# Mixer of a two-block network on one core: two z gate units laid between the levels, their gate function in the inverse

## The chip, the core and the metric

One NeuronCore of one Trainium2 chip. The metric is the device time of one launch in microseconds. Everything runs in one program on five engines: TensorE (PE), VectorE (DVE), ScalarE (ACT), GpSimd (POOL) and SyncE (SP), which issues the weight transfers.

## The reference

A first block of two layers (swiglu, attention of several kinds, memory attention, swiglu), which the change leaves alone, and a second block of two layers, each a mixer and a convolved gated feed-forward, on 256 tokens of width 1024, all in float32. The mixer, cut to what matters here:

```
p = h @ w_in                                   # qkv, z, beta, a, hq, hf, hi, hgate, gate_dn, gate_hg
o_dn = delta_rule(q, k, v, beta, g) forward + backward      # chunked; the triangular inverse t_inv of (a + eye)
o_dn = rmsnorm(o_dn) * dn_norm * silu(z)
o_hg = hgrn2(silu(hq), kk, hi, logf) forward + backward     # decays over all pairs of tokens
o_hg = rmsnorm(o_hg) * hg_norm * silu(hgate)
merged = sigmoid(gate_dn) * (o_dn @ w_branch_dn) + sigmoid(gate_hg) * (o_hg @ w_branch_hg)
return merged @ w_out
```

## The kernel before

**Weights** come as a stream of 324 units of 1 MB (128 x 2048 floats) through a ring of three slots. Every unit is split in two halves: ScalarE rounds a half into `w_hi` (`split_half`, L1340), VectorE subtracts it from the original into `ring_lo` (L1813), and TensorE multiplies high by high, high by low and low by high: 48 matmuls of 256 columns a unit. `feed(u)` on either engine splits unit u+2. ScalarE may write half h of unit u+2 only when TensorE has consumed half h of unit u; SyncE loads unit u+3 when unit u is used up. `features` (L754) yields columns turned, half by half; `tokens` (L767), used for hi, hz and z, needs both halves.

**Banks.** Results land in four PSUM banks taken in turn. A tile is opened only when the tile four before it has been read (`take` on ScalarE, L1305; `gather`, `conv_qkv` and others on VectorE). The order of tiles is written by `Plan.stages` and must be the order in which TensorE makes them.

**The mixer** (`mixer2`, once in each engine's program, l = 0 and 1). Each engine runs its list in the order of the text; semaphores join them. TensorE's order:

- projections: qkv and hf in turn, hq, hi, hz (hgate); then the square sums of q and k (L1125) and the sums of the decays (L1133); then the two z units. ScalarE takes z through silu (`silu_tokens`, L1624).
- the levels k = 0 to 8 (`LEVELS` is 7): for each k, VectorE builds two exponent arguments (`args(l, k)`, L2301 and L2303) over 1024 columns each, ScalarE exponentiates (L1634), GpSimd multiplies with the queries (`qmul`, L2692), TensorE multiplies per head (L1078), VectorE puts the result where a mask says (`gather`, L2332). Beside each level runs a part of the delta rule's preparation (`prepare(k)`): decay rows at 0 and 1, the Gram matrix at 2 (L2419), k and v turned at 3 (`kv_T`, L1088), query-key products at 4 (L2428). GpSimd masks matrices in `decays_of` (L2697, L2698) and `masked` (L2704), and multiplies hz and z by their norm gains (`row_gains`, L2682). Between levels one gate unit is laid (`GATE_AT`), eight in all, split in halves.
- the substitution: the inverse of the 16 x 16 diagonal blocks, in 14 rows one after the other. `near_start` on VectorE sums strided columns (L2435, four instructions) and starts it; `near_row(c)` on TensorE (L1159) and `near_step(c)` on VectorE (L2447, L2448) alternate, each waiting for the other. Rows lie after halves of gate units from (3, 0) on and after levels 4 to 8. `level_masks(NEAR)` on GpSimd waits for `near_start`.
- the inverse by levels 4 to 6: W0, Y and Z (L1078, L2490). At the last one ScalarE applies the sigmoid to the gates (L1761, 4096 columns). Then the state chain, `branch_hg` (L1269), `branch_dn`, `out_proj`.

`near_start` stands at `half == 1 and k == 2`: after `gather(2)`, the Gram products, `args(l, 4)` and one split, ahead of `gather(3)`. `args(l, 1)` stands after the split for hz1.

## Time and profile before

| | us |
|---|---|
| median of 3 runs | 2311.51 |
| lowest, highest | 2311.47, 2316.66 |
| the profiled execution | 2303.78 |
| its span | 2301.6 |
| TensorE busy | 2184.7 |
| VectorE busy | 1566.2 |
| ScalarE busy | 1064.4 |
| GpSimd busy | 191.6 |

Busy times are of the whole span, most of which the change does not touch. The two mixers' level loops lie at 1380 to 1473 us and 1898 to 1991 us. An engine's idle time in a row is followed by the instruction that ended it.

### The profile page before, as it was taken

To read this page: it belongs to the slowest core of one execution; us is meant where nothing else is said; L and a number is where in the kernel's file an instruction comes from. 1 tells how busy PE (TensorE), PEld (TensorE's weight loads), DVE (VectorE), ACT (ScalarE), POOL (GpSimd) and SP (SyncE) were. 2 spreads that over 40 slices of the span, in tenths; PEclk is the share of its full clock that TensorE was granted. 3 is DMA by queue.
4 is the path that set the end of the run, shared out by engine and by line. 5 is a ranking of instruction groups with operands and counts; after the bars stand their busy time and mean duration, and the time that the engine had idled before them with its cause. 6 is when DMAs were issued, how large, how long until landed. Compare 5 with 4: busy or idle time off the path is not lost.

```text
span 2301.6 us, 39173 instructions
## 1 busy us (share of the span) xinstructions
PE 2184.7 (95%) x15722; PEld 2038.9 (89%) x15722; DVE 1566.2 (68%) x2330; ACT 1064.4 (46%) x1504; POOL 191.6 (8%) x157
## 2 busy tenths in 40 slices
PE   7999989999999999999998998999999998999997
PEld 7998859989999998798997988898998988898996
DVE  4557657656575575667556689867767689867676
ACT  4335465533353345554333475434434475434442
POOL 0000000131000000000001007300000007300000
PEclk9999999999999999999999999999999999999999
DMA  6554424475555554344553442214554442214553
GB/s 251 188 182 165 165 74 165 153 214 184 208 194 187 188 191 146 128 147 166 185 191 139 165 147 92 74 56 149 190 189 167 165 147 92 74 62 168 183 183 126
DMA packets 52665, 359.10 MB, mean 156 GB/s; under 512 B 6400, under 2 KB 6784, under 8 KB 11072
## 3 DMA queue, kind: packets, MB, share of 16 engines
q1 hardware_dynamic: 46928, 340.81, 41.3%
q0 software_dynamic: 4336, 13.37, 2.1%
q10 hardware_dynamic: 1280, 3.19, 0.4%
q8 instruction: 91, 1.49, 0.3%
q14 instruction: 30, 0.25, 0.0%
HBM read 356.29 MB, written 1.05 MB: 155 GB/s over the span
## 4 chain that ended last, share of the span: by engine, by line
PE 79%; DVE 11%; ACT 4%; DMA 4%; issue 2%; SPq 0%; DVEq 0%; POOLq 0%; ACTq 0%
PE tile L754 43%; PE acc L787 18%; PE tile L767 7%; PE tile L1078 3%; DMA ring<-weights 3%; DVE ring_lo L1813 2%; PE tile L1269 2%; ACT w_hi L1340 2%; PE tile L923 1%; PE tile L897 1%; PE tile L802 1%; DVE work L2332 1%; DVE work L2303 1%; DVE bn L2198 0%; DVE work L2301 0%
## 5 line engine op out<-in xcount | busy, mean ns | idle before, releaser
L1813 DVE TENSOR_TENSOR ring_lo<-ring,w_hi 128x1024 fp32r<-128x1024 f32 x648 | 788.6, 1247 | 594.1 <-ACT w_hi L1340 591.9
L1340 ACT ACTIVATE w_hi<-ring 128x1024 fp32r<-128x1024 f32 x648 | 657.7, 1053 | 913.8 <-DMA ring<-weights 706.2
L754 PE MATMUL tile<-xT_hi,w_hi 128*128 128x256 f32 x3008 | 859.3, 286 | 25.7 <-DVE xT_lo L1804 13.9
L754 PE MATMUL tile<-xT_lo,w_hi 128*128 128x256 f32 x3008 | 854.2, 284 | 0.0
L754 PE MATMUL tile<-xT_hi,ring_lo 128*128 128x256 f32 x3008 | 854.0, 284 | 0.0
L754 PEld LDWEIGHTS tile<-xT_hi,w_hi 128*128 128x128 f32 x3008 | 580.3, 193 | 33.7 <-DVE ring_lo L1813 17.0
L754 PEld LDWEIGHTS tile<-xT_lo,w_hi 128*128 128x128 f32 x3008 | 580.5, 193 | 2.1
L754 PEld LDWEIGHTS tile<-xT_hi,ring_lo 128*128 128x128 f32 x3008 | 580.2, 193 | 0.0
L787 PE MATMUL acc<-w_hi,hidden_hi 128*128 128x512 f32 x528 | 206.6, 391 | 2.0 <-DVE ring_lo L1813 2.0
L787 PE MATMUL acc<-w_hi,hidden_lo 128*128 128x512 f32 x528 | 206.1, 390 | 0.0
L787 PE MATMUL acc<-ring_lo,hidden_hi 128*128 128x512 f32 x528 | 205.5, 389 | 0.0
L1305 ACT ACTIVATE work<-tile 128x512 f32<-128x512 f32 (+2 forms) x186 | 101.0, 566 | 64.2 <-PE tile L1078 28.6
L1078 PE MATMUL tile<-work 128*128 128x128 f32 (+1 forms) x976 | 117.2, 280 | 3.8 <-issue 1.6
L1078 PEld LDWEIGHTS tile<-work 128*128 128x128 f32 x976 | 114.3, 195 | 5.0 <-issue 3.7
L787 PEld LDWEIGHTS acc<-w_hi,hidden_hi 128*128 128x128 f32 x528 | 99.4, 188 | 21.5 <-issue 2.2
L787 PEld LDWEIGHTS acc<-ring_lo,hidden_hi 128*128 128x128 f32 x528 | 99.2, 188 | 21.1
L787 PEld LDWEIGHTS acc<-w_hi,hidden_lo 128*128 128x128 f32 x528 | 99.4, 188 | 18.3
L767 PE MATMUL tile<-w_hi,xT_hi 128*128 128x256 f32 x352 | 100.2, 285 | 7.1 <-ACT work L1611 3.2
L767 PE MATMUL tile<-w_hi,xT_lo 128*128 128x256 f32 x352 | 99.6, 283 | 0.0
L767 PE MATMUL tile<-ring_lo,xT_hi 128*128 128x256 f32 x352 | 99.6, 283 | 0.0
L787 PE MATMUL acc<-w_hi,xT_hi 128*128 128x512 f32 x192 | 77.4, 403 | 2.8 <-DVE xT_lo L1804 2.8
L767 PEld LDWEIGHTS tile<-w_hi,xT_hi 128*128 128x128 f32 x352 | 67.5, 192 | 8.3 <-issue 5.0
(273 smaller groups left out, 2718.1 us busy)
## 6 DMA issues: line engine op xcount, KB each, us to landing
ring<-weights SPq DMA_DIRECT2D x324, 1024.0 KB, 4.8
work<-ln_g_rows POOLq DMA_DIRECT2D x8, 512.0 KB, 6.0
work<-ln_b_rows POOLq DMA_DIRECT2D x8, 512.0 KB, 7.2
work<-rpb POOLq DMA_DIRECT2D x32, 96.0 KB, 13.7
x<-x_in SPq DMA_DIRECT2D x1, 1024.0 KB, 8.0
work<-mem_in ACTq DMA_DIRECT2D x1, 1024.0 KB, 6.6
out<-x POOLq DMA_DIRECT2D x1, 1024.0 KB, 4.4
work<-hmask_in ACTq DMA_DIRECT2D x1, 840.0 KB, 8.3
```

Of the source, the lines that this page charges most:

```text
L754: j = mm(ps[:, f * S:(f + 1) * S], w[a][:, k, :], x2[b][:, k, :], start=(k == 0 and i == 0), stop=(k == KT - 1 and i == 2))
L767: j = mm(ps[:, tt * 256:(tt + 1) * 256], x2[b][:, k, tt * P:(tt + 1) * P], w[k // 4][a][:, k % 4, :], start=(k == 0 and i == 0), stop=(k = ...
L787: j = mm(acc[b][:, :], src[d][:, at + k, (b // 2) * P:(b // 2 + 1) * P], w[k][c][:, 0, (b % 2) * 512:(b % 2 + 1) * 512], start=(first and ...
L802: i = nc.tensor.transpose(ps[:, k * S + tt * P:k * S + (tt + 1) * P], src[:, tt, c:c + P], ident)
L897: i = mm(ps[:, tt * S:(tt + 1) * S], qs[m][:, tt * P:(tt + 1) * P], ks[m], start=(m == 0), stop=(m == len(qs) - 1))
L923: i = mm(dst, value_rows(a, e, j)[:, st, :], probT[:, e % 4, st, :], start=(st == 0), stop=(st == TT - 1))
L1078: i = mm(part(ps[:, h * P:(h + 1) * P]), lhsT(h), rhs(h), start=True, stop=True)
L1269: i = mm(ps[:, f * S:(f + 1) * S], w[c][:, k, f * P:(f + 1) * P], x2[d][:, 2 * q0 + k, :], start=(k + p == 0), stop=(k == 3 and p == 2))
L1305: A(dst, ps[:, :] if src is None else src(ps), ACT.Copy, scale=scale).then_inc(tile_taken[t % NB], 1)
L1340: A(high_of(u, h), half_of(ring, u, h), ACT.Copy).then_inc(sems["w_hi"], 1)
L1813: V.tensor_tensor(half_of(ring_lo, u, h), half_of(ring, u, h), high_of(u, h).bitcast(F32), ALU.subtract).then_inc(sems["w_lo"], 1)
L2303: V.tensor_tensor(half(Q), pairs_of(hX, 0, m, n + m), pairs_of(hX, m, m, n - 1, 0), ALU.subtract).then_inc(sems["hg_arg"], 1)
```

## The change

- The z units leave the place ahead of level 0. z0 is laid behind gate unit 2, z1 behind gate unit 5 (`Z_AT`), in the weight stream, the plan of tiles and on all engines.
- ScalarE only copies z (`take`); silu is applied to both at once, 1024 columns, in the last level of the inverse, ahead of the sigmoid. GpSimd's gains of z wait for it and come last.
- The square sums and decay sums come after hi, ahead of hz; ScalarE squares before it takes hi0. VectorE reads the decay sums before the split for hz0, scales q and k before that for hz1, and does `args(l, 1)` after it.
- `near_start` comes at `half == 0 and k == 3`, behind `gather(3)` and `args(l, 5)`. Row 1 comes after (3, 1) in place of (3, 0); the row so lost comes after z1 (`NEAR_AFTER_Z`).

```diff
-             ("hi", 0), ("hi", 1), ("hz", 0), ("hz", 1), ("z", 0), ("z", 1))
+             ("hi", 0), ("hi", 1), ("hz", 0), ("hz", 1))
-NEAR_AFTER_HALF = ((3, 0), (3, 1), (4, 0), (4, 1), (5, 0), (5, 1), (6, 0), (6, 1), (7, 0))
+Z_AT = {2: 0, 5: 1}
+NEAR_AFTER_Z = (5,)
+NEAR_AFTER_HALF = ((3, 1), (4, 0), (4, 1), (5, 0), (5, 1), (6, 0), (6, 1), (7, 0))
...
@@ TensorE
-                for name in ("hi", "hz"):
-                    for j in range(2):
-                        project(name, j)
+                for j in range(2):
+                    project("hi", j)
                 square_sums()
                 decay_sums()
                 for j in range(2):
-                    project("z", j)
+                    project("hz", j)
...
+                    if k in Z_AT:
+                        project("z", Z_AT[k])
+                    if k in NEAR_AFTER_Z:
+                        near_row(next(rows))
...
@@ ScalarE
-                for j in range(2):
-                    feed_one("hi", j)
-                    if j == 0:
-                        silu_qkv(5)
-                    take(T[("hi", l, j)], tok2(hi, j))
+                feed_one("hi", 0)
+                silu_qkv(5)
                 act.wait_ge(sems["qkv_silu"], 6 * l + 4)
                 for j in range(4):
                     A(pair(l2s, j), pair(qkvT, j), ACT.Square).then_inc(sems["l2_sq"], 1)
-                for j in range(2):
-                    feed_one("hz", j)
-                    silu_tokens(T[("hz", l, j)], tok2(hz, j))
+                take(T[("hi", l, 0)], tok2(hi, 0))
+                feed_one("hi", 1)
+                take(T[("hi", l, 1)], tok2(hi, 1))
...
                 for j in range(2):
-                    feed_one("z", j)
-                    silu_tokens(T[("z", l, j)], tok2(zs, j))
+                    feed_one("hz", j)
+                    silu_tokens(T[("hz", l, j)], tok2(hz, j))
...
+                    if k in Z_AT:
+                        feed_one("z", Z_AT[k])
+                        t = T[("z", l, Z_AT[k])]
+                        take(t, tok2(zs, Z_AT[k]), lambda ps: ps.rearrange("p (t c) -> p t c", t=TT))
...
                     if v == LEVELS - 1:
+                        for j in range(2):
+                            act.wait_ge(*taken(T[("z", l, j)]))
+                        A(zs, zs, ACT.Silu).then_inc(sems["z_silu"], 1)
                         for i in range(8):
                             act.wait_ge(*taken(T[("gate", l, i)]))
                         A(gates[:, :, :], gates[:, :, :], ACT.Sigmoid).then_inc(sems["gates_ready"], 1)
...
@@ VectorE
                 feed_one("hi", 1)
                 next(parts)
-                feed_one("hz", 0)
-                next(parts)
-                feed_one("hz", 1)
-                args(l, 1)
...
+                next(parts)
+                feed_one("hz", 0)
                 for j in range(4):
                     dve.wait_ge(sems["l2_inv"], 4 * l + j + 1)
                     V.tensor_tensor(pair(qkvT, j), pair(qkvT, j), pair(l2s, j), ALU.mult).then_inc(sems["l2_done"], 1)
-                feed_one("z", 1)
+                feed_one("hz", 1)
+                args(l, 1)
...
-                        if half == 1 and k == 2:
+                        if half == 0 and k == 3:
                             near_start()
...
+                    if k in Z_AT:
+                        feed_one("z", Z_AT[k])
+                    if k in NEAR_AFTER_Z:
+                        near_step(next(rows))
...
@@ GpSimd
+                    if name == "z":
+                        pool.wait_ge(sems["z_silu"], l + 1)
...
                 qmul(6)
-                row_gains("z", zs, 0)
                 qmul(7)
                 qmul(8)
                 level_masks(NEAR + 1)
                 level_masks(NEAR + 2)
+                row_gains("z", zs, 0)
```

## Rows read from the trace of the kernel before

**Rows 1.** The page: the chain that ended last, by engine, shares of the span.
```profile
PE 79%; DVE 11%; ACT 4%; DMA 4%; issue 2%; SPq 0%; DVEq 0%; POOLq 0%; ACTq 0%
```

**Rows 2.** TensorE's waits in 1897:1991: total, times, longest us.
```profile
PE tile L1088 <- DVE work L2332: 6.1, 1, 6.1
PE acc L1159 <- DVE work L2448: 3.5, 3, 1.6
PE tile L754 <- DVE work L2332: 2.9, 2, 2.3
```

**Rows 3.** Busy sums, level 0 to gate unit 6, both mixers; columns as headed.
```profile
core 0: us, PE busy (x) PEld busy (x) DVE busy (x) ACT busy (x) POOL busy (x), PEclk, DMA share, GB/s
1380.10:1454.40 74.30, 63.61 (x516) 62.65 (x515) 68.65 (x69) 40.37 (x55) 50.03 (x25) 0.95 0.28 98
1897.90:1972.40 74.50, 62.75 (x515) 61.79 (x515) 68.15 (x69) 40.40 (x55) 49.99 (x25) 0.95 0.28 98
```

**Rows 4.** The same columns for three stretches at a low clock.
```profile
1408.30:1411.70 3.40, 3.40 (x18) 3.40 (x17) 2.98 (x5) 0.00 (x0) 3.40 (x4) 0.50 0.00 0
1500.40:1507.30 6.90, 6.90 (x35) 6.90 (x35) 2.72 (x11) 2.68 (x5) 0.00 (x0) 0.51 0.01 2
1937.30:1944.20 6.90, 4.27 (x20) 4.28 (x21) 6.87 (x7) 1.20 (x2) 6.03 (x4) 0.51 0.01 2
```

**Rows 5.** First mixer: z in the chain (start, us); ScalarE's and TensorE's timeline.
```profile
1368.64 11.62 PE tile L767 x96
...
1348.55 0.63 ACT L1629 ACTIVATE work<-work 128x512 f32<-128x512 f32 x1 [0.16 <-DVEq L2188]
1351.37 2.01 ACT L1340 ACTIVATE w_hi<-ring 128x1024 fp32r<-128x1024 f32 x2 [1.71 <-DMA ring<-weights]
1353.76 2.18 ACT L1694 ACTIVATE l2s<-work 128x512 f32<-128x512 f32 x4
1366.55 2.42 ACT L1702 ACTIVATE l2s<-tile,small 128x512 f32<-128x512 f32 x4
...
1367.38 1.03 PE L1133 MATMUL tile<-small,const 128*128 128x4 f32 x8 [0.34 <-ACT l2s L1702]
```

**Rows 6.** VectorE's timeline in the second mixer: start, us, line, operands, count.
```profile
1898.37 2.36 DVE L1813 TENSOR_TENSOR ring_lo<-ring,w_hi 128x1024 fp32r<-128x1024 f32 x2 [1.35 <-ACT w_hi L1340]
1903.37 3.75 DVE L2303 TENSOR_TENSOR work<-work 128x1024 f32<-128x1024 f32 x1
...
1957.14 1.21 DVE L2301 TENSOR_TENSOR work<-work 128x1024 f32<-128x1024 f32 x1
...
1964.96 3.42 DVE L2301 TENSOR_TENSOR work<-work 128x1024 f32<-128x1024 f32 x1
```

**Rows 7.** GpSimd's timeline there; its first 12 rows have no gap.
```profile
1903.07 2.97 POOL L2692 TENSOR_TENSOR work<-work 128x1024 f32<-128x1024 f32 x1 [38.42 <-ACT work L1634]
...
1926.61 6.50 POOL L2704 TENSOR_TENSOR work<-work,blocks 128x512 f32<-128x512 f32 x4
1938.17 7.39 POOL L2704 TENSOR_TENSOR work<-work,blocks 128x512 f32<-128x512 f32 x4 [1.18 <-DVE work L2439]
1952.35 2.39 POOL L2692 TENSOR_TENSOR work<-work 128x1024 f32<-128x1024 f32 x1 [6.79 <-ACT work L1634]
```

**Rows 8.** VectorE's strided sums and gather(3), and TensorE's transposes and gate units.
```profile
1925.19 0.36 PE L754 MATMUL tile<-xT_hi,w_hi 128*128 128x256 f32 x1 [2.26 <-DVE work L2332]
1934.10 3.77 DVE L2435 TENSOR_REDUCE work<-work 128x64 f32<-128x512 f32 x4
1939.14 1.34 DVE L2332 COPY_PREDICATED work<-hmask,tile 128x512 f32<-128x512 uint8 x2
1939.93 1.97 PE L1088 MATMUL tile<-const,work 128*128 128x128 f32 x8 [6.09 <-DVE work L2332]
1941.55 0.56 PE L754 MATMUL tile<-xT_hi,w_hi 128*128 128x256 f32 x1
1959.97 0.46 PE L1159 MATMUL acc<-work,spread_own 128*128 128x96 f32 x2 [1.10 <-DVE work L2448]
```

**Rows 9.** ScalarE and TensorE at the end of the second mixer's inverse.
```profile
2025.12 1.28 ACT L1761 ACT_TABLE_LOAD   x1
2026.42 3.62 ACT L1761 ACTIVATE work<-work 128x4096 f32<-128x4096 f32 x1
2029.94 0.58 ACT L1305 ACTIVATE work<-tile 128x512 f32<-128x512 f32 x1
...
2030.62 0.35 PE L1078 MATMUL tile<-work 128*128 128x128 f32 x1 [0.79 <-issue]
```

More of the change, by code:

```diff
@@ L261, in stages @@
                     self.from_chip(("ba_T", l), 1)
-                if (name, j) == ("hz", 1):
+                if (name, j) == ("hi", 1):
                     self.from_chip(("l2", l), 4)
@@ L270, in stages @@
                     self.from_units(("gate", l, k), 1)
+                if k in Z_AT:
+                    self.from_units(("z", l, Z_AT[k]), 1)
             self.from_chip(("hg_o", l), 2)
@@ L387, in weight_stream @@
         out += [packed[name][j:j + 1] for name, j in PROJECTED]
-        out.append(pack_features(w[:, 4624:6672]))
+        gates = pack_features(w[:, 4624:6672])
+        for k in range(8):
+            out.append(gates[k:k + 1])
+            if k in Z_AT:
+                out.append(packed["z"][Z_AT[k]:Z_AT[k] + 1])
         out.append(pack_branch(a["w_branch_hg_2"][l]))
@@ L581, in build @@
                   "a_scaled", "a_ready", "a_near", "a_level", "near_eye", "spread", "near_x", "near_row", "x_first", "vb", "kd", "nbe",
-                  "z_ready", "dn_ssq", "dn_std", "dn_out", "gates_ready", "merged_dn", "merged"]
+                  "z_ready", "z_silu", "dn_ssq", "dn_std", "dn_out", "gates_ready", "merged_dn", "merged"]
         qs_both = region(0, 2, 4 * S)
@@ L1742, in mixer2 @@
                             take(T[("gate", l, g)], pair(gates, g))
+                    if k in Z_AT:
+                        feed_one("z", Z_AT[k])
+                        t = T[("z", l, Z_AT[k])]
+                        take(t, tok2(zs, Z_AT[k]), lambda ps: ps.rearrange("p (t c) -> p t c", t=TT))
                 for g in range(4):
@@ L2398, in mixer2 @@
                 signal(sems["gc_arg"], 1)
-                feed_one("z", 0)
+                next(parts)
+                feed_one("hz", 0)
                 for j in range(4):
@@ L2471, in mixer2 @@
                                                 ALU.mult).then_inc(sems["x_first"], 1)
+                    if k in Z_AT:
+                        feed_one("z", Z_AT[k])
+                    if k in NEAR_AFTER_Z:
+                        near_step(next(rows))
                 dve.wait_ge(*ready(T[("hg_o", l)] + 1))
```

## The prediction

> **What bounds the kernel now.** I read the page first: TensorE is busy for 2184.7 of 2301.6 us, and the chain that ended last is 79% TensorE and 11% VectorE [rows 1]. Work taken from other engines is therefore worth nothing unless TensorE waits for it; the question is where TensorE stands still inside the two mixers. The matmuls of the z units are not removed, only laid elsewhere, so a gain can come only from idle time of TensorE that they fill. The list of waits over the level loop of the second mixer gives that idle time: 6.1 us in one wait before the third kv transpose, 2.9 us in two waits before gate units, 3.5 us in three waits before rows of the substitution, 12.5 us in all, every one ended by VectorE [rows 2]. The first mixer has 5.0 in place of 6.1 and else the same. Then the sums by stretch: from the first matmul of level 0 to the first of gate unit 6 takes 74.3 us and 74.5 us; VectorE is busy 68.7 and 68.2 of them, GpSimd 50.0 [rows 3]. So this stretch belongs to VectorE as much as to TensorE: what is put into it must fit VectorE too. Last the clock: after such idle time TensorE is granted 0.5, its 1.2 GHz level in place of 2.4, for 3.4 us in gate unit 2 of the first mixer, which has only a wait of 2.3 us ahead of it, and for 6.9 us around the long wait of the second [rows 4]. At 1.2 GHz gate unit 3's first half in the second mixer lost 1.2 us.
>
> All times below are in the second mixer, counted from level 0's first matmul at 1897.86; the first differs by tenths. Each term falls twice.
>
> **What moves out in front.** A z unit is 48 matmuls; two are 11.6 us (96 in 11.62) [rows 5]. They leave the place ahead of level 0 and their 11.6 us come back inside the loop, so the loop's stretch must grow by less than 11.6 us for a gain.
>
> **The square sums go earlier: +0.6.** They now stand behind hi, with hz behind them. ScalarE, from its silu at 1349.18: squares 2.18 (to 1351.4), take hi0 0.58, split for hi1 2.01, take hi1 0.58 (1354.5), table load 1.28, first logarithm 0.6 (1356.4). TensorE ends hi1 at 1351.9 and the squares 3.6 us later at 1355.5, then waits 0.9 us for that bank; today this wait is 0.34 us [rows 5]. Cost 0.6 us. The split of the next weights stays hidden: the two hz units (11.6 us) lie over it.
>
> **The level exponents' first arguments go later: +1.2 at gate unit 2.** `args(l, 1)` was done long before level 0; now it follows the split of hz1, which ends 2.9 us after that unit's last matmul (z1 today: 1897.86 to 1900.73), and gather(0) stands behind it [rows 6]. Two instructions of 1.21 us put gather(0) from 2.8 to 5.2, so gate unit 0, which needs the bank that the gather empties, starts at 5.9 in place of 5.3. The exponent follows at 5.2 and the first product on GpSimd at 7.2 in place of 5.2. GpSimd then has no gap for 30 us [rows 7], and VectorE's two-input operations come out at 2.1 to 3.8 us instead of 1.21 wherever one of GpSimd's runs [rows 6, 7]. I carry 1.2 of the 2.0 us to gate unit 2 (bounds 0 and 2.0; the gather that releases it is behind VectorE work which has slack of about 0.8): it starts at 28.6 in place of 27.3.
>
> The Trainium skill (SBUF — State Buffer, "two separate sides") says that a VectorE operation with two SBUF inputs and a GpSimd operation exclude each other for the whole instruction. The trace agrees: the 3.75 us instruction ends 1.1 us after GpSimd's 2.97 us product. By that rule alternate operations, not shares of bandwidth, set the times of the next steps; I had the same from the rows.
>
> **z0 behind gate unit 2.** Gate 2 ends at 34.4, z0 at 40.2. Its bank is free. VectorE's split ends 2.9 later (43.1), gather(3) empties its first bank at 43.8 and ends at 44.5; the third kv transpose goes at 43.9, gate unit 3 at 45.0 against 43.7 today [rows 8]. So z0 is hidden but for 1.3 us: the 6.1 us wait is filled. This is the change's gain.
>
> **The strided sums behind gather(3): +1 more.** Today the four reductions (3.77 us) and a small subtraction stand before gather(3), under that wait; row 1 never waited. Now gather(3) ends at 44.5, args(5) is blocked once by the product of level 4 (2.2) and takes 2 x 1.2: 49.1; sums and subtraction 3.96: 53.0. TensorE is through gate 3 at 50.8 and waits 2.2 us at row 1. Level 4 starts at 53.3 against 51.0. If args(5) is not blocked there is no wait here; if both halves are, it is 4.4.
>
> **VectorE from there on.** The mask products of GpSimd (7.39 us for four) wait for those sums, so they now fall on splits and steps that ran undisturbed: split 1.2, step 1.4, split 2.1, gather 0.7 give gate unit 4 at 58.4 against 54.8. Behind the masks come level 5's product and the gains of hz (2.4 us each), over args(6), which ran free (1.21 each) [rows 6, 7]: rest of gather 0.65, step 1.0, QK products 2.5, args(6) 4.6, step 0.5: 67.6. Row 4, now at the end of gate 4, waits for that, 3.2 us, against 1.1 us today; gate 5 starts at 69.7 against 64.4. The z gains no longer fall on args(7) (3.42 us today, 1.21 free), which gives back 2.2 us of VectorE time.
>
> **z1 behind gate unit 5.** VectorE is by now behind, so little is idle to fill: gate 5 with rows 6 and 7 and 1.0 us of wait ends at 76.8, z1 at 82.6, level 6 and its row at 84.6 to 85.4, where the row waits 0.9 us for the split of z1 and the added step behind it. Gate unit 6 starts at 86.4. Against 74.5 that is 11.9 more; less the 11.6 us that left: **+0.3**. Bounds by the rows: no collision at all takes off 1.2, 2.2, 2.2 and 1.4 (about -6.5), two at each place add as much as 3.
>
> **Clock: +0.8.** The long wait goes, and with it 1.2 us lost at 1.2 GHz (2.0 in the first mixer), which is counted above as gained; but waits of 3.1 (gate 2), 2.2 and 3.2 us take its place, and 2.3 us was enough once of two times [rows 2, 4]. A fall costs 1.4 us (half of 3.4 us at half speed, less a little). Bounds 0 and 3; I take 0.8.
>
> **The silu in the inverse: +2.35.** z is now only copied; a silu over 1024 columns stands before the sigmoid of the gates. Today ScalarE, after its last take of Y, loads a table (1.28), does the sigmoid (3.62) and takes the first new rows (ends at 2030.52), and TensorE's next group starts at 2030.62 after 0.79 us of idle [rows 9]. ScalarE is already last there, so all that is added is on the path. Silu: 1.06 by the rows of other 128x1024 activations. A load of its own: every change between two such functions in the trace has one of 1.28 us, so 2.34. Bounds 1.06 (both in one table) and 2.34. What follows up to the branch is one serial chain, so nothing takes it back. GpSimd's z gains (2.4 us) now run there too and hold VectorE until about the same moment; nothing more.
>
> The Trainium skill (ScalarE: Activation LUTs, "What ACT_TABLE_LOAD costs", and its rule to batch by table set) speaks against this edit: a switch is 1.28 us plus a drain of 1.38. The trace shows the 1.28 and no drain: the sigmoid starts 0.02 us after the load. By the page the term would be 3.7 and the sum 2.8 us larger for the two mixers.
>
> **Sum.** 0.6 + 0.3 + 0.8 + 2.35 = 4.05 us a mixer, 8.1 in all. The profiled execution took 2303.8 us (span 2301.6): 2311.9. The median of the runs is 7.7 us above the profiled one; on it the forecast is **2319.6 us**. A measurement tells a change from none at about 0.3%, 7 us, so this is just on the slow side; its own range is 2314 to 2326.
>
> **Rivals.**
> 1. Faster: the gaps are really filled. If args(5), args(6) and the splits miss GpSimd's operations, the loop gains 6.5 in place of losing 0.3, and the clock stays up: 0.6 - 6.5 + 2.35 = -3.6 a mixer: 2304.4. For it: 12.5 us of waits stand there, and it needs about half of them; from 3 us on it is a gain. Against: VectorE's 68 of 74 us. It decides at row 1: a wait under 0.5 us there. Chance 0.17.
> 2. No difference: the loop comes out even, the clock stays up, and silu shares the sigmoid's table: 0.6 + 0.3 + 1.06 = 2: 2315.5. Against the last: three loads for sqrt, sigmoid, sqrt. Chance 0.30.
> 3. Slower, the clock: it falls at gate 2, at row 4 and behind the lengthened wait in the inverse (0.79 + 2.35 = 3.1 us), where the first mixer already spent 6.9 us at 0.5 [rows 4]: 1.4 + 1.4 + 1.7 more: 8.1 + 9 = 17: 2328.5. Chance 0.13.
> Forecast 0.40.
>
> Range 2303 to 2330. Slower by over 0.3% (above 2318.4): 0.6 of the forecast, rival 3, a little of rival 2: 0.42. Faster (below 2304.6): most of rival 1: 0.15. Within: 0.43.
>
> **What would show it.** Right: no wait of 5 us before the kv transposes; a wait of about 2 us for VectorE at the first row and 3 us at the fourth; level 0 to gate 6 at about 86 us; in the inverse two table loads, and the idle time before the first state product at about 3.1 us. Wrong: an idle time there under 1 us (then silu is hidden), or the loop at 80 us (then z1 was hidden too).

## The result, and the profile after

The changed kernel takes 2325.45 us in the median of 10 runs (2316.64 to 2336.84), the kernel before beside it 2311.49 us (10 runs, 2304.35 to 2316.66). The ratio is 1.0063, interval 1.0048 to 1.0078: slower by 14 us, between 11 and 18. The forecast was 8.1 us slower, 2319.6 us. The direction and the serial costs were right; 6 us are missing from the sum, and by an estimate from all runs they belong to the clock of TensorE.

The profiled executions differ by more: the span went from 2301.6 to 2324.0 us. The windows of both mixers show where. The first fence is the kernel after, in three stretches of each mixer (from hi to level 0; level 0 to gate unit 6; gate unit 6 to `branch_hg`), and ahead of them the stretch up to the first mixer's hi. Columns as in [rows 3]. In the changed kernel the line numbers are others: L762 are the gate units, L1096 the transposes, L1167 the rows of the substitution, L1086 the products of levels and states; on VectorE L2344 and L2347 are the gathers, L2451 the end of `near_start`, L2460 `near_step`.

```profile
0.00:1348.80 1348.80, 1291.93 (x9031) 1194.66 (x9031) 835.30 (x1259) 624.37 (x938) 55.73 (x85) 0.98 0.50 171
1377.40:1463.10 85.70, 74.71 (x611) 73.08 (x610) 75.05 (x76) 45.22 (x61) 49.00 (x23) 0.98 0.30 106
1463.10:1541.00 77.90, 71.82 (x565) 70.55 (x564) 51.74 (x97) 29.94 (x37) 18.06 (x11) 0.91 0.09 33
1903.30:1989.20 85.90, 74.66 (x611) 73.04 (x610) 75.01 (x76) 45.25 (x61) 48.96 (x23) 0.98 0.29 107
1989.20:2064.60 75.40, 69.09 (x564) 67.83 (x564) 51.50 (x97) 29.68 (x36) 18.07 (x11) 0.95 0.09 33
```

The kernel before, in the stretches that [rows 3] do not hold:

```profile
0.00:1340.30 1340.30, 1279.39 (x9030) 1186.32 (x9030) 834.87 (x1259) 624.19 (x938) 57.39 (x85) 0.99 0.49 172
1340.30:1380.10 39.80, 39.42 (x307) 37.21 (x308) 31.61 (x50) 29.09 (x43) 0.40 (x1) 1.00 0.43 157
1454.40:1527.50 73.10, 69.18 (x565) 67.85 (x564) 50.32 (x98) 27.44 (x34) 16.03 (x10) 0.95 0.09 32
1972.40:1990.50 18.10, 17.29 (x141) 17.04 (x141) 16.37 (x26) 5.47 (x5) 8.16 (x5) 1.00 0.18 66
1990.50:2042.20 51.70, 48.57 (x426) 47.53 (x425) 33.95 (x72) 21.64 (x29) 7.85 (x6) 1.00 0.06 22
```

- Ahead of the mixer no instruction is changed, and yet 1348.8 stands against 1340.3 us, with 12.5 us more of busy TensorE for the same matmuls: in that execution 51 us ran at the 1.2 GHz level, in the one before 24. In the 13 profiled executions of this study the stretch takes 1340.3 to 1346.8 us with the old order of the weights (3 of them) and 1340.5 to 1352.2 with the new, and on the whole it is the longer the more of it runs at 1.2 GHz (24 us in the shortest, 55 in the longest). So these 8.4 us are a difference of the clock between two executions; that the change adds to it is not shown, and the runs of the table behind experiment 8 speak against it.
- hi to level 0: 28.64 us against 39.75, which is +0.5 once the 11.6 us of z are added. The second mixer has 30.11 against 39.83, +1.9; a stretch of 3.4 us at 1.2 GHz lies in it.
- Level 0 to gate unit 6: +11.4 in both mixers against [rows 3], less the 11.6 that left: -0.2.
- Gate unit 6 to `branch_hg`: 77.85 against 73.09, and 75.37 against 69.82 us: +4.8 and +5.5.

The mixers lose 5.1 and 7.3 us, 12.3 us together, and 10.3 of it in the inverse. Another 1.7 us lie between the mixers, where after has 3.4 us at 1.2 GHz.

The inverse holds falls of the clock that the change did not bring. 44 to 45 us into the stretch TensorE waits 0.78 us for VectorE in every kernel, and up to 2.6 us later the clock falls in 18 of the 26 profiled mixers, for 6.8 or 10.2 us: in before in the first mixer ([rows 4], 1500.4) and not in the second, in after in both. They are as frequent with the silu ahead of the sigmoid (7 of 10) as without (11 of 16). Without a fall the stretch takes 69.7 to 69.8 us. Each us at 1.2 GHz costs 0.42 to 0.48 us in it, so such a fall is worth 3.2 to 3.3 us or 4.9. The one of after's first mixer:

```profile
1508.90:1515.70 6.80, 6.80 (x34) 6.80 (x34) 2.83 (x11) 2.25 (x5) 0.00 (x0) 0.50 0.01 2
```

TensorE's waits in the second mixer's loop (after), beside [rows 2]: the wait of 6.1 us before the third kv transpose is down to 0.7, and the waits have moved to the rows of the substitution.

```profile
PE acc L1167 <- DVE work L2460: 5.3, 3, 3.3
PE tile L762 <- DVE work L2347: 3.3, 2, 2.5
PE acc L1167 <- DVE work L2451: 1.9, 1, 1.9
PE tile L762 <- DVE work L2344: 0.9, 1, 0.9
PE tile L1096 <- DVE work L2347: 0.7, 1, 0.7
```

The timeline of after: row 1, row 4 and the first state product; then ScalarE ahead of that product. These answer to [rows 8] and [rows 9].

```profile
1957.60 0.41 PE L1167 MATMUL acc<-work,spread_own 128*128 128x32 f32 x2 [1.86 <-DVE work L2451]
1971.34 0.45 PE L1167 MATMUL acc<-work,spread_own 128*128 128x80 f32 x2 [3.31 <-DVE work L2460]
2053.01 0.46 PE L1086 MATMUL tile<-work 128*128 128x128 f32 x2 [3.16 <-issue]
...
2045.15 1.28 ACT L1773 ACT_TABLE_LOAD   x1
2046.44 1.06 ACT L1773 ACTIVATE work<-work 128x1024 f32<-128x1024 f32 x1
2047.52 1.28 ACT L1776 ACT_TABLE_LOAD   x1
2048.81 3.62 ACT L1776 ACTIVATE work<-work 128x4096 f32<-128x4096 f32 x1
2052.33 0.58 ACT L1316 ACTIVATE work<-tile 128x512 f32<-128x512 f32 x1
```

The wait of 3.16 us is [rows 9]'s 0.79 plus 2.37, a table load and a silu.

### The profile page after: what moved, and what is told of

Its sections match the earlier page's. It is cut to its first block, busy times and chain, and to the rows that moved or that the text cites. A ratio compares the mean times of both kernels' runs of the same rounds, so it can differ in the third digit from the quotient of the medians.

```text
span 2324.0 us, 39179 instructions
## 1 busy us (share of the span) xinstructions
PE 2206.1 (95%) x15722; PEld 2054.7 (88%) x15722; DVE 1567.8 (67%) x2330; ACT 1069.2 (46%) x1508; POOL 191.9 (8%) x157
## 4 chain that ended last, share of the span: by engine, by line
PE 77%; DVE 12%; DMA 5%; ACT 5%; issue 2%; SPq 0%; POOLq 0%; DVEq 0%; ACTq 0%
PE tile L762 43%; PE acc L795 19%; PE tile L775 4%; DMA ring<-weights 4%; PE tile L1086 3%; DVE ring_lo L1828 3%; ACT w_hi L1351 2%; PE tile L1280 2%; PE tile L931 1%; PE tile L905 1%; DVE work L2316 1%; PE tile L810 1%; DVE work L2318 1%; PE tile L918 1%; DVE bn L2213 1%
## 5 line engine op out<-in xcount | busy, mean ns | idle before, releaser
L762 PE MATMUL tile<-xT_hi,w_hi 128*128 128x256 f32 x3008 | 858.8, 286 | 25.2 <-DVE xT_lo L1819 13.9
L762 PE MATMUL tile<-xT_lo,w_hi 128*128 128x256 f32 x3008 | 854.5, 284 | 0.0
L762 PE MATMUL tile<-xT_hi,ring_lo 128*128 128x256 f32 x3008 | 854.5, 284 | 0.0
L762 PEld LDWEIGHTS tile<-xT_hi,w_hi 128*128 128x128 f32 x3008 | 580.4, 193 | 32.2 <-DVE ring_lo L1828 15.7
L762 PEld LDWEIGHTS tile<-xT_lo,w_hi 128*128 128x128 f32 x3008 | 580.4, 193 | 2.2
L762 PEld LDWEIGHTS tile<-xT_hi,ring_lo 128*128 128x128 f32 x3008 | 580.3, 193 | 0.0
L1316 ACT ACTIVATE work<-tile 128x512 f32<-128x512 f32 (+1 forms) x190 | 103.9, 567 | 72.5 <-PE tile L1086 31.1
L1086 PE MATMUL tile<-work 128*128 128x128 f32 (+1 forms) x976 | 122.5, 287 | 8.3 <-issue 6.3
L1086 PEld LDWEIGHTS tile<-work 128*128 128x128 f32 x976 | 119.6, 203 | 9.5 <-issue 8.4
L795 PE MATMUL acc<-w_hi,xT_hi 128*128 128x512 f32 x192 | 77.4, 403 | 0.0
```

The costliest lines, as they stand in the source:

```text
L762: j = mm(ps[:, f * S:(f + 1) * S], w[a][:, k, :], x2[b][:, k, :], start=(k == 0 and i == 0), stop=(k == KT - 1 and i == 2))
L795: j = mm(acc[b][:, :], src[d][:, at + k, (b // 2) * P:(b // 2 + 1) * P], w[k][c][:, 0, (b % 2) * 512:(b % 2 + 1) * 512], start=(first and ...
L1086: i = mm(part(ps[:, h * P:(h + 1) * P]), lhsT(h), rhs(h), start=True, stop=True)
L1316: A(dst, ps[:, :] if src is None else src(ps), ACT.Copy, scale=scale).then_inc(tile_taken[t % NB], 1)
```

## The experiments

Each was timed in 3 to 5 rounds against the kernel before. "Ahead" is the stretch up to hi, "clean" a stretch without time at 1.2 GHz.

**1. The change once more.** No edit.

> The changed kernel once more, unedited. In its first profile 12.3 us of the 22.4 us of longer span lay inside the two mixers (5.0 and 7.3 from the first hi unit to branch_hg) and 8.4 us ahead of them, in code that the change does not touch. Theory A (the mixers' serial work costs the time): the mixers again take 5 to 7 us each more than before, and the stretch ahead of the first mixer comes out within 2 us of the kernel before. Rival B (something in the unchanged part is slower for good, as by the other order of the weights): 8 us ahead of the mixers again. Total by A +10 to +15, by B +20.

Ratio 1.0041 (1.0025 to 1.0058), 2323.5 us. Ahead 1345.9 us, where theory A wanted 1340.3 within 2 us and rival B 8 us more: it fits neither, which suits a length that the clock sets anew each time. The mixers take +2.8 and +7.5 us against before; the first lacks the fall of 6.8 us behind the long wait that after had. The waits in the loop are the same but for row 4 (2.6 us in the first mixer, and 0.6 before gate unit 4). So the loss in the mixers repeats, within some us of the clock, and the loss ahead of them does not keep its size.

**2. Silu behind the take.** The three lines move from the last level of the inverse to between the takes of `vnA` and `vnB`, when the state products already run.

```diff
                     if v == LEVELS - 1:
-                        for j in range(2):
-                            act.wait_ge(*taken(T[("z", l, j)]))
-                        A(zs, zs, ACT.Silu).then_inc(sems["z_silu"], 1)
                         for i in range(8):
...
                 take(T[("vnA", l)], vn[:, 0, :])
+                for j in range(2):
+                    act.wait_ge(*taken(T[("z", l, j)]))
+                A(zs, zs, ACT.Silu).then_inc(sems["z_silu"], 1)
                 take(T[("vnB", l)], vn[:, 2, :])
```

> The silu over z moved on ScalarE from ahead of the sigmoid to behind the take of vnA, where ScalarE was idle for 5.6 us in the kernel before. Theory A: the wait before the first state product goes back from 3.16 us to 0.79, 2.4 us a mixer, and with it the fall of the clock behind it (up to 3 us more in a mixer that had one): 5 to 9 us faster than the changed kernel. Rival C (GpSimd's z gains and the idle time elsewhere take its place): the gap falls, but branch_hg does not start earlier by more than 1 us a mixer; under 3 us in all.

2312.59 us, ratio 0.9997 (0.9983 to 1.0011): 10.9 us less than experiment 1 on the same chip, a little more than the 5 to 9 expected. ScalarE and TensorE around that point; the load and the silu are still there, and TensorE's wait is back at 0.79:

```profile
1520.77 0.58 ACT L1316 ACTIVATE work<-tile 128x512 f32<-128x512 f32 x1
1521.37 1.28 ACT L1777 ACT_TABLE_LOAD   x1
1522.66 1.06 ACT L1777 ACTIVATE work<-work 128x1024 f32<-128x1024 f32 x1
1526.93 0.60 ACT L1316 ACTIVATE work<-tile 128x512 f32<-128x512 f32 x1 [3.21 <-PE tile L1086]
...
1521.45 1.24 PE L1086 MATMUL tile<-work 128*128 128x128 f32 x9 [0.79 <-issue]
```

In the kernel before, ScalarE was idle for 5.6 us there, and with load and silu it is still idle for 3.2, so the same work costs nothing. The place of one activation was the difference between slower and equal in the medians. Of the 10.9 us the wait explains 4.7; experiment 4 takes up the rest.

**3. The strided sums ahead of gather(3) again.** Beside it everything of the change.

```diff
-                        if half == 0 and k == 3:
+                        if half == 1 and k == 2:
                             near_start()
```

> The strided sums back at level 2, ahead of gather(3), everything else as changed. Theory A: the wait of 1.86 us at row 1 goes, GpSimd's mask products start 10 us earlier and no longer run beside the splits and args(6), so the 3.31 us wait at row 4 shrinks below 1.5; gather(3) comes at most 1.5 us later. Level 0 to gate unit 6 from 85.7 to about 82 us, 3 to 4 us a mixer, 6 to 8 us in all. Rival D (the sums had to go behind the gather because z0's place leaves no room ahead): the kv transposes wait about 4 us in place of 0.7 and the stretch stays at 85 us or grows.

2316.8 us, ratio 1.0023 (1.0007 to 1.0038), 6.7 us less than experiment 1. The loop is 81.7 and 82.6 us in place of 85.7 and 86.0. The waits of the first mixer's loop:

```profile
PE tile L762 <- DVE work L2347: 3.3, 2, 2.5
PE acc L1167 <- DVE work L2460: 2.1, 2, 1.1
PE tile L1096 <- DVE work L2347: 1.2, 1, 1.2
PE tile L762 <- DVE work L2344: 0.9, 1, 0.9
```

Row 1's wait (1.86) is gone and row 4's is 1.1 in place of 3.3; the kv transposes wait 1.15 in place of 0.70. The sums could have stayed: z0's matmuls over them left room for 3.8 us. Moving them behind the gather bought 0.4 us and cost 3.4 to 4. VectorE's busy time in the loop fell from 75.05 to 73.47 us in the first mixer and from 75.01 to 74.19 in the second, so 0.8 to 1.6 us are operations that run shorter; the rest is order.

**4. Silu alone, in the kernel before.** z is copied, its silu stands ahead of the sigmoid, GpSimd's gains come last; the z units stay ahead of level 0. A second kernel has the silu where experiment 2 puts it.

```diff
-                    silu_tokens(T[("z", l, j)], tok2(zs, j))
+                    take(T[("z", l, j)], tok2(zs, j), lambda ps: ps.rearrange("p (t c) -> p t c", t=TT))
...
                     if v == LEVELS - 1:
+                        for j in range(2):
+                            act.wait_ge(*taken(T[("z", l, j)]))
+                        A(zs, zs, ACT.Silu).then_inc(sems["z_silu"], 1)
...
-                row_gains("z", zs, 0)
                 qmul(7)
...
+                row_gains("z", zs, 0)
```

> The kernel before with one part of the change alone: z copied, the silu over both z units in the inverse ahead of the sigmoid, GpSimd's z gains last; z units stay ahead of level 0. Theory A: the wait before the first state product grows from 0.79 to 3.16 us in both mixers, 4.7 us in all, plus what a fall of the clock adds there (0 to 3 us a mixer), less about 1 us a mixer of the level loop because the z gains leave args(7) alone: +3 to +8 us against the kernel before. Rival C: within 2 us of the kernel before.

> The kernel before with z copied and its silu behind the take of vnA; z units stay ahead of level 0, sums as before. Theory A: the level loop stays at 72 us as in the run with the silu ahead of the sigmoid (2.3 us under the kernel before, because GpSimd starts earlier without the two table loads at z and the z gains leave args(7)), and the wait before the state product is back at 0.79: 2 to 2.5 us a mixer, 4 to 5 us below the kernel before. It says how much of any gain has nothing to do with the place of the z units. Rival F (those 2.3 us come from the clock): 0.

2316.45 us, ratio 1.0020 (1.0001 to 1.0039), wait 3.16 us; with the silu late 2312.87, ratio 0.9995 (0.9985 to 1.0006), wait 0.79. The first is within the expected +3 to +8; the second missed its 4 to 5 us of gain.

That expectation was read across a border. The loop, level 0 to gate unit 6, was 72 us in both, 2.4 less than before. But the kernel before waits 1.64 us for a row of the substitution just ahead of gate unit 6, and these two wait 0.91 us behind the first half of that unit instead, which is in the next stretch. Without a fall of the clock the next stretch takes 70.9 us in the kernels with that wait, and 69.8 in before. In experiment 8, second mixer:

```profile
1971.10:2042.00 70.90, 66.06 (x565) 64.58 (x564) 51.45 (x98) 30.83 (x37) 18.02 (x11) 1.00 0.11 44
```

So 1.1 of the 2.4 us only changed stretches. Of the 1.3 that remain, 0.8 are there at gate unit 2 already (26.5 us after level 0 in place of 27.3), far ahead of the gains of z: a silu at z needed a table load ahead of it and one behind it, the copy needs none, and the first exponent comes earlier. (The whole kernel has 38 loads with the silu ahead of the sigmoid, 40 before.) The second kernel's profiled execution spent 10.2 us at 1.2 GHz in each inverse besides.

Three pairs now differ in the place of the silu alone: 1.0041 to 0.9997, 1.0020 to 0.9995, and 1.0023 to 0.9976 (experiment 3 and 5). Their mean is 0.39% or 9.0 us, about 6 to 12, where the lengthened waits account for 2 x 2.37 = 4.7.

The granted clock at the end of that wait tells of the rest. Windows of this kernel (silu ahead of the sigmoid), one in each mixer; the wait ended at 1520.34 and 2042.96:

```profile
1520.50:1523.90 3.40, 3.40 (x17) 3.40 (x17) 0.69 (x1) 0.00 (x0) 0.00 (x0) 0.50 0.00 0
2042.70:2046.10 3.40, 3.14 (x15) 3.17 (x16) 0.69 (x1) 0.16 (x1) 0.00 (x0) 0.50 0.00 0
```

The kernel after, first mixer, there (the wait ended at 1526.91):

```profile
1525.90:1532.70 6.80, 5.79 (x27) 5.82 (x28) 2.15 (x5) 0.91 (x2) 0.00 (x0) 0.50 0.00 1
```

Experiment 2, both mixers, from the start of its wait of 0.79 us on, over 10.8 us:

```profile
1520.60:1531.40 10.80, 9.69 (x82) 9.32 (x82) 7.66 (x24) 4.97 (x6) 2.36 (x1) 1.00 0.01 2
2038.20:2049.00 10.80, 9.69 (x82) 9.32 (x82) 7.66 (x24) 4.98 (x6) 2.36 (x1) 1.00 0.01 2
```

Over all profiled executions: from the end of the wait of 3.16 us on (at most 1.0 us sooner) the clock stood at 1.2 GHz in 6 of 10 mixers (4 times for 3.4 us, 2 times for 6.8), behind the wait of 0.79 us in none of 16. The cost is what the stretch takes beyond a clean one (69.8 or 70.9 us), the 2.37 us and the earlier fall: 74.73 - 70.9 - 2.37 = 1.5 us in the first mixer of this kernel, 1.4 to 1.5 in the three others with 3.4 us, 2.5 in the first of after. That is 1.1 us a mixer in the mean, and the deferred silu comes to 2 x (2.37 + 1.1) = 6.9 us, which the 6 to 12 allow. The 2 us up to 9.0 are within the interval and have no cause shown.

**5. Both repairs.** Experiments 2 and 3 in one kernel.

> The changed kernel with both earlier edits at once: silu behind the take of vnA, strided sums back ahead of gather(3). Theory A (two separate serial costs): level 0 to gate 6 about 82 us as with the sums alone, gate 6 to branch_hg about 70 to 73 as with the silu alone, so each mixer 4 us shorter than with the silu alone: 184 and 183 us, against 187.2 and 184.2 of the kernel before. Total 3 to 6 us below the kernel before. Rival E (the clock takes it back): the sum of the two gains, 11 and 7 us, does not appear, since falls of the clock just move; within 2 us of the kernel before.

2307.99 us, ratio 0.9976 (0.9961 to 0.9991): with the silu late and the sums early, the kernel is 4.4 us faster than before in the medians, as theory A expected. In the profile the first mixer took 183.4 us, as forecast; the second 189.0, with 20.5 us at 1.2 GHz in it.

**6. The arguments of level 1 ahead of the split for hz1.** First in the changed kernel, then in experiment 5's.

```diff
-                feed_one("hz", 1)
                 args(l, 1)
+                feed_one("hz", 1)
```

> The changed kernel with args(l, 1) ahead of VectorE's split for hz1, nothing else. Theory A (my step of the prediction: 0.6 us at gate 0, 1.2 us by gate 2): the wait before gate 0 goes from 0.85 to 0, gate unit 2 starts 1 to 1.5 us earlier after level 0, level 0 to gate 6 from 85.8 to about 84.6; 2 to 3 us in all below the changed kernel. Rival G: under 1 us, as the waits before gates 1 and 2 grow in its place (they did, by 0.6 and less, where the sums were early too).

> As the run with both edits, and args(l, 1) ahead of VectorE's split for hz1. Theory A: gather(0) comes 2.4 us earlier, the 0.9 us wait before gate 0 goes, GpSimd starts 1.3 to 2 us earlier; 1 us a mixer, 2 us in all, below the run with both edits. Rival G (gate 2 is released by VectorE's own work): the wait before gate 0 goes and the one before gate 2 grows by as much; within 1 us.

2322.98 us (1.0037; 1.0025 to 1.0049), which is not to be told from experiment 1, as rival G had it; and 2302.52 us (0.9964; 0.9950 to 0.9978), 5.5 us less than experiment 5. What the loop shows is smaller: the wait at gate unit 0 is gone (0.85 to none), but where gate 1 still waits it is 1.4 to 1.5 in place of 0.85, and gate unit 2 starts at 28.0 in place of 28.8 in the first one's second mixer. From hi to gate unit 6 that is 109.8 us against 110.4 in the first mixers, 111.3 against 112.9 in the second. So the order is worth 0.5 to 1.6 us a mixer. Of the rest the clock has a part: the runs of this kernel spent 7 us less at 1.2 GHz than those of experiment 5 (table below), which is worth 2 us.

**7. z1 ahead of level 0.** On top of experiment 6's second kernel: z1 is projected after hz1, as before, z0 stays behind gate unit 2, and the rows have their old places. One thing more differs, which "as that run" in the expectation passes over: `args(l, 1)` stands where the kernel before has it, behind the split for hz1 and ahead of the one for z1.

```diff
-Z_AT = {2: 0, 5: 1}
-NEAR_AFTER_Z = (5,)
-NEAR_AFTER_HALF = ((3, 1), (4, 0), ...
+Z_AT = {2: 0}
+NEAR_AFTER_Z = ()
+NEAR_AFTER_HALF = ((3, 0), (3, 1), (4, 0), ...
...
@@ VectorE
-                args(l, 1)
                 feed_one("hz", 1)
+                args(l, 1)
+                feed_one("z", 1)
```

> As that run, but z1 stays ahead of level 0 and only z0 lies in the loop; the rows of the substitution lie as in the kernel before. Theory A (behind gate 5 VectorE is the bound and z1 fills nothing): 5.8 us move from the loop to the stretch ahead and the mixer keeps its length within 1 us, or gets shorter by up to 2. Rival H (z1 does fill the 1.64 us wait that stood there): 1.6 us a mixer longer.

> The kernel with z1 ahead and z0 behind gate 2 once more, for a second measurement beside the run with both in the loop: 0.995 to 0.997 of the kernel before, mixers of 182 to 184 us in the profile apart from falls of the clock.

2304.51 us, ratio 0.9957 (0.9941 to 0.9973), and once more 2302.55 us, 0.9955 (0.9939 to 0.9971). The first mixer of the first one, hi to level 0 and level 0 to gate unit 6, both clean:

```profile
1347.10:1381.50 34.40, 33.65 (x259) 31.41 (x260) 29.40 (x48) 26.36 (x40) 0.40 (x1) 1.00 0.41 151
1381.50:1454.80 73.30, 66.51 (x564) 65.55 (x563) 69.34 (x71) 41.58 (x58) 48.36 (x23) 1.00 0.30 103
```

Together 107.7 us, where z1 behind gate unit 5 made 109.8. But not these 2.1 us are z1's. The wait of 0.91 us before a row falls behind the border here, as in experiment 4, and takes 1.1 us with it into the next stretch. And gate unit 2 starts 27.3 us after level 0, as in the kernel before, in place of 28.2; the arguments stand a unit further ahead of level 0 here. From hi to `branch_hg`, with a clean inverse, it is 178.6 us here (178.9 and 179.8 in two mixers with 3.4 us at 1.2 GHz in the loop) against 179.5 there, also with 3.4 us: the mixer keeps its length within 1 us, as theory A had it, and which of the two places is better for z1 is not shown. VectorE is busy for 69.3 of the loop's 73.3 us here.

z0 is the part that pays. The second kernel of experiment 4 has both z units in front (39.92 + 71.87 = 111.8) and the same border; against it 3 to 4 us a mixer are gone (the two differ in z0's place and the orders in front).

**8. z0 behind gate unit 1, z1 behind gate unit 2.** Again on top of experiment 6's second kernel, with its order of the arguments and splits; neither z unit stands in front.

```diff
-Z_AT = {2: 0, 5: 1}
-NEAR_AFTER_Z = (5,)
-NEAR_AFTER_HALF = ((3, 1), (4, 0), ...
+Z_AT = {1: 0, 2: 1}
+NEAR_AFTER_Z = ()
+NEAR_AFTER_HALF = ((3, 0), (3, 1), (4, 0), ...
```

> With the silu late, the sums early and args(l, 1) early: z0 behind gate unit 1 and z1 behind gate unit 2, rows as in the kernel before. GpSimd, not VectorE or TensorE, paces levels 0 to 3 (no gap in its work for 30 us), so a unit there costs only VectorE's two splits. Theory A: the waits before gate 2 (2.26 us) and the kv transposes (1.3 to 2.8) are filled by z0, stretch hi to gate 6 from 107.9 us (z1 ahead) to about 105.5: 2 us a mixer, 4 in all, below the kernel with z1 ahead. Rival H: VectorE's splits of z0 meet GpSimd's operations at 2.1 us each, gather(2) and with it gate 2 come 4 us later, and nothing or less than nothing is left of it.

2304.84 us, ratio 0.9958 (0.9940 to 0.9975). The second mixer, hi to level 0 and level 0 to gate unit 6, and its waits in the loop:

```profile
1865.10:1893.70 28.60, 27.84 (x210) 25.61 (x211) 24.98 (x45) 23.96 (x37) 0.40 (x1) 1.00 0.40 142
1893.70:1971.10 77.40, 72.40 (x611) 71.43 (x611) 75.55 (x75) 44.02 (x61) 48.73 (x23) 1.00 0.33 111
```

```profile
PE tile L1096 <- DVE work L2347: 2.7, 1, 2.7
PE acc L1167 <- DVE work L2460: 1.9, 2, 1.0
PE tile L762 <- DVE work L2347: 1.3, 1, 1.3
```

106.0 us, 1.7 less than in experiment 7: the wait of 2.3 us ahead of gate unit 2 is filled, while the kv transposes still wait 2.7. VectorE is busy for 75.6 of 77.4 us, so there is little left to fill. The 4 us in all that theory A expected did not come: in the medians the two cannot be told apart.

**All runs, with their clock.** Each run's span and mean granted clock c are on record, and 2 x (1 - c) x span is its time at 1.2 GHz. In the 190 runs, a us more of that time goes with 0.31 us more of span within a kernel (a line through the runs of each, with one slope for all; 0.30 in the 77 runs of before alone). That takes a difference apart: "at equal clock" is what remains when 0.31 us for each us at 1.2 GHz is taken off; it is an estimate, good to about 1.2 us. An asterisk marks mixers in which 1.1 us lie behind the border at gate unit 6.

| kernel | ratio to before | us at 1.2 GHz, mean of the runs | us against before, at equal clock | profile: hi to gate unit 6, first and second mixer (us at 1.2 GHz) |
|---|---|---|---|---|
| before | 1 | 77 | 0 | 114.1 (6.8), 114.4 (6.8) |
| after | 1.0063 | 92 | +8.6 | 114.4 (3.4), 116.1 (6.8) |
| 1, after again | 1.0041 | 84 | +7.9 | 114.6 (3.4), 116.3 (6.8) |
| 2, silu late | 0.9997 | 67 | +2.9 | 114.8 (3.4), 117.3 (10.2) |
| 3, sums early | 1.0023 | 87 | +2.1 | 110.3 (3.4), 112.7 (6.8) |
| 4, z in front, silu ahead of the sigmoid | 1.0020 | 85 | +3.2 | 111.8 (6.8)*, 112.2 (6.8)* |
| 4, z in front, silu late | 0.9995 | 84 | -2.2 | 111.8 (6.8)*, 111.8 (6.8)* |
| 5, both | 0.9976 | 75 | -3.8 | 110.4 (3.4), 112.9 (6.8) |
| 6, after with the arguments early | 1.0037 | 87 | +6.4 | 113.4 (6.8), 118.1 (13.7) |
| 6, both and the arguments early | 0.9964 | 68 | -5.7 | 109.8 (3.4), 111.3 (6.8) |
| 7, z1 ahead | 0.9957 | 71 | -7.6 | 107.7 (0)*, 108.1 (3.4)* |
| 7, again | 0.9955 | 70 | -7.1 | 108.9 (3.4)*, 109.2 (3.4)* |
| 8, z behind 1 and 2 | 0.9958 | 78 | -8.9 | 107.6 (3.4)*, 106.0 (0)* |

The kernels of experiments 5, 6 (its second), 7 and 8 beat both kernels, by 0.2 to 0.4% on the one before. The silu's three pairs differ by 5.0, 5.4 and 5.9 us at equal clock (the waits: 4.7), and by 17, 0.5 and 12 us at 1.2 GHz.

## Why the prediction was right, and where its size was off

- **z0 hidden but for 1.3 us; the long wait filled.** Right in the mechanism: the kv transposes wait 0.7, and the value of z0 there is 3 to 4 us a mixer (experiment 7). Gate unit 3 started at 46.5 (45.0 forecast, 43.7 before); the 1.5 us are a fall of the clock in gate unit 2, 3.4 us long.
- **The square sums, +0.6.** Right: +0.5 in the clean front; their bank's wait is 0.7.
- **Gate unit 2 at 28.6.** Measured 28.8, behind a wait of 2.5 us (3.1 forecast). Gate unit 0 started at 6.4 (5.9 forecast). The arguments' own part of it was less than the 1.2 us forecast: putting them early gave back 0.6 to 0.8 at gate unit 2 (experiment 6).
- **Row 1 waits 2.2, row 4 3.2, row 9 0.9.** Measured 1.86, 3.31 and 0.97 to 1.17. Row 4 started at 68.0 (67.6 forecast), gate unit 6 at 85.7 and 86.0 (86.4). The loop's +0.3 was -0.2. (The bound of this step with no collision, "about -6.5", adds up to 0.3 - 7.0 = -6.7; nothing hangs on it.) The alternation of GpSimd's and VectorE's two-input operations, from which these followed, shows in the fence below this list: the first half of `args(5)` took 3.25 us beside a product of GpSimd, the second, of the same shape and free of it, 1.21. The Trainium skill (SBUF — State Buffer, "two separate sides") gives the exclusive lock as the reason; the trace agrees in these two numbers. How much of experiment 3's 4 us comes from such meetings is not shown apart from the 0.8 to 1.6 us by which VectorE's busy time fell.
- **The silu, +2.35.** The wait grew by 2.37, and all of it was on the path. The Trainium skill (ScalarE: Activation LUTs, "What ACT_TABLE_LOAD costs") would have added a drain of 1.38 us; here each function started 0.01 to 0.02 us after its load of 1.28, and the wait has no room for a drain. The prediction also had the rule of the Trainium skill to batch by table set (ScalarE: Activation LUTs, "Table sets: the hidden batching unit") speak against this edit. The count of loads says otherwise: with the silu deferred and nothing else changed there are 38, against 40 before, one less in each mixer. What cost was the place of the load and the silu, ahead of a product that waits for ScalarE; experiment 2 has both and no such wait.
- **The step that failed: the size of "Clock: +0.8".** The prediction counted 1.2 us (2.0 in the first mixer) of the long wait's fall as gained in the loop and put 0.8 us for new falls beside it, all in the loop; for the inverse it said that nothing more comes. In the loop that was not too little: there was one stretch of 3.4 us a mixer, less than before's 6.8. What the runs showed in its place are falls elsewhere. In the inverse the wait of 3.16 us is followed by 1.2 GHz in 6 of 10 mixers, worth 1.1 us a mixer. The forecast had this only in its third rival, at 1.7 us, with a chance of 0.13; for this place it was the likelier case. And in the front of the second mixer the clock fell for 3.4 us in 6 of the 8 kernels with both z units out of it, +1.5 us, not foreseen. The price of a fall was right: 1.4 us for 3.4 us forecast, 1.4 to 1.5 measured.
- **The sum with these sizes:** 8.1 - 1.6 (the clock of the loop) - 1.0 (the loop, twice 0.5) + 2.2 (the inverse) + 1.5 (the front) = 9.2 us. Experiment 1, the second measurement of the same kernel, gave 9.5 us (6 to 13); the first gave 11 to 18.
- **Where the rest of the 14 us lies.** In the clock, by the estimate in the table above. At equal clock the change costs 8.6 and 7.9 us in its two measurements, which is what its serial costs add up to: front 0.5, loop -0.2 and about 1.4 more for its 3.4 us less at 1.2 GHz, silu 2.37, twice: 8.1. The forecast without its clock had nearly the same, 2 x (0.6 + 0.3 + 1.2 + 2.35) = 8.9, with the 1.2 us counted as gained put back, so it took the clock to give back 0.8 us in all. Instead the runs of after spent 15 us more at 1.2 GHz than those of before, worth 4.7 us, and those of experiment 1 spent 7 us more, worth 2.2. That the forecast's 8.1 and this 8.1 are the same number is in part luck, since one has the clock in it and the other has not.
- **What stays open.** Where all of that time at 1.2 GHz lies. The profiles show 5.4 us of it behind the long wait and 2.6 in the front (means over the mixers), less 3 to 7 in the loop, and the two means of ten runs, 15 and 7 us above before, are uncertain by 5 and 3 us. Nor does a run here show why the clock falls at 44 us in some inverses and not in others, the kernel before included.

VectorE's two halves of `args(5)` in the second mixer of after, and GpSimd's product over the first:

```profile
1949.16 3.25 DVE L2316 TENSOR_TENSOR work<-work 128x1024 f32<-128x1024 f32 x1
1952.34 1.21 DVE L2318 TENSOR_TENSOR work<-work 128x1024 f32<-128x1024 f32 x1
...
1948.94 2.40 POOL L2710 TENSOR_TENSOR work<-work 128x1024 f32<-128x1024 f32 x1 [6.93 <-ACT work L1645]
```

First rival (gaps really filled): it was to be decided by row 1's wait, and fell with 1.86 us there; experiments 5 to 8 are that rival, brought about by other edits. Second rival: its shared table is refuted by two loads. That the new order of the weights slowed the unchanged part (rival B of experiment 1) fell too: experiment 4 has the old order and 1346.8 us ahead of hi, experiment 6's second kernel the new one and 1340.5, and over all runs the kernels of experiments 2, 6 (second) and 7 have the new order and spend less time at 1.2 GHz than before (67 to 71 against 77 us).

## What to carry to other kernels

Price each edit of a bundle at its own place: here one edit (z0 in the longest wait) was worth 3 to 4 us a mixer, two others (the strided sums, the silu) cost 3.4 to 4 each, and the sum told nothing of the first. A small instruction moved onto an engine that ends last just before a serial chain costs its full length and can cost the clock behind it as well; look a few instructions further down for a place where that engine waits. Before a difference of two stretches is believed, look whether a wait has only crossed the border between them, and take the clock out of it. Work that fills a gap of the bounding engine pays only where the gap is, so lay it at the longest wait and leave the orders of the other engines there alone.

## What the runs showed of the hardware

- An idle time of 3.16 us of TensorE was followed by the 1.2 GHz level in 6 of 10 cases, one of 0.79 us in none of 16, at the same place of the same chain. The length of the idle time does not decide alone: 14 to 20 us earlier in the same inverse a wait of 0.78 us was followed by that level, within 2.6 us, in 18 of 26 cases.
- A us at 1.2 GHz cost 0.42 to 0.48 us in the inverse, and 0.31 us over the whole kernel (190 runs).
- The same unchanged 1340 us ran between 24 and 58 us at 1.2 GHz from one execution to the next and took 1340.3 to 1352.2 us: a single profile of this kernel can mislead by as much as the whole change was worth. The fronts of the mixers, where they were free of it, agreed within 0.3 us between kernels of one order.
- A table load of 1.28 us started 0.01 to 0.02 us after the activation ahead of it, and the next activation 0.01 to 0.02 us after the load.
